# FFN 1's second pair as eight products, setup stores behind the next pair, rescaling on ScalarE, three low parts on Pool

## The reference, cut to what matters

```python
def rmsnorm(x, g):
    return x * lax.rsqrt(jnp.mean(x * x, axis=-1, keepdims=True) + NORM_EPS) * g

def swiglu(x, w_gate, w_up, w_down):
    return (jax.nn.silu(x @ w_gate) * (x @ w_up)) @ w_down

x = x + 0.5 * swiglu(rmsnorm(x, p['g_ffn1']), p['ffn1_gate'], p['ffn1_up'], p['ffn1_down'])
```

## Time and profile before

| | us |
|---|---|
| median of 3 runs | 2503.97 |
| lowest and highest | 2502.36, 2505.84 |
| the profiled execution | 2505.05 |
| its span, first to last instruction | 2503.3 |
| first FFN, pairs 0 to 21 | 8.58 to 551.17 |
| its down side | 552.63 to 808 |

### The profile page before, as it was taken

One profiled execution on the slowest core, in us unless ns is written; L12 is line 12 of the kernel. 1 busy time (PEld: TensorE's weight loads), 2 busy tenths in 40 slices (PEclk: granted clock), 3 DMA queues, 4 the chain that ended last, 5 costly groups with the idle time before them and its releaser, 6 DMA issues. The chain is left out here.

```text
span 2503.3 us, 51841 instructions
## 1 busy us (share of the span) xinstructions
PE 2390.7 (96%) x21940; PEld 2332.1 (93%) x21940; DVE 1441.7 (58%) x1993; ACT 708.5 (28%) x1347; POOL 1193.3 (48%) x761
## 2 busy tenths in 40 slices
PE   7988988899999999999998999999999999999998
PEld 7988988889999999999997888799999999999997
DVE  7787767698226445473357667666754444453225
ACT  6322222230102000011244666522433333341001
POOL 5665666564444334422341000234677778775550
PEclk9999999999999999999999999999999999999998
DMA  5211222243323352543362110054222222153211
GB/s 195 88 68 67 76 76 76 76 185 130 104 78 126 111 119 85 179 89 86 117 202 97 32 33 19 3 211 146 77 85 76 76 76 76 67 186 112 74 51 69
DMA packets 104135, 243.89 MB, mean 97 GB/s; under 512 B 17240, under 2 KB 43480, under 8 KB 103328
## 3 DMA queue, kind: packets, MB, share of 16 engines
q1 hardware_dynamic: 76560, 190.72, 22.8%
q10 hardware_dynamic: 27408, 50.76, 6.4%
HBM read 174.47 MB, written 65.82 MB: 96 GB/s over the span
## 5 line engine op out<-in xcount | busy, mean ns | idle before, releaser
L172 POOL TENSOR_TENSOR whi<-wraw,small 128x1024 fp32r<-128x1024 f32 (+1 forms) x60 | 103.4, 1724 | 418.4 <-PE ps L206 340.1
L921 PE MATMUL ps<-t_hi,whi 128*128 128x258 f32 x688 | 151.5, 304 | 54.5 <-POOL wlo L494 25.7
L206 PE MATMUL ps<-hhi,whi 128*128 128x344 f32 x816 | 177.4, 326 | 0.0
L206 PE MATMUL ps<-hlo,whi 128*128 128x344 f32 x816 | 174.0, 322 | 0.0
L206 PE MATMUL ps<-hhi,wlo 128*128 128x344 f32 x816 | 173.7, 322 | 0.0
L921 PEld LDWEIGHTS ps<-t_hi,whi 128*128 128x128 f32 x688 | 116.2, 207 | 58.9 <-POOL wlo L494 28.7
L494 POOL TENSOR_TENSOR wlo<-weights_sum,whi 128x512 fp32r<-128x512 f32 x63 | 85.8, 1363 | 135.8 <-ACT whi L761 135.1
L921 PE MATMUL ps<-t_lo,whi 128*128 128x258 f32 x688 | 148.1, 299 | 0.0
L175 POOL TENSOR_TENSOR wlo<-wraw,whi 128x1024 fp32r<-128x1024 f32 (+1 forms) x60 | 145.0, 2416 | 4.7
L921 PE MATMUL ps<-t_hi,wlo 128*128 128x258 f32 x688 | 147.2, 297 | 0.0
L3916 PE MATMUL ps<-t_hi,whi 128*128 128x258 f32 x704 | 143.8, 285 | 3.0 <-ACT ffn_gate L3823 1.0
(11 more groups left out here) (587 smaller groups left out, 6890.7 us busy)
## 6 DMA issues: line engine op xcount, KB each, us to landing
weights_raw_b<-ffn_up SPq DMA_DIRECT2D x22, 1024.0 KB, 5.0
wraw<-ffn_up SPq DMA_DIRECT2D x21, 1024.0 KB, 5.0
a_spilled<-ffn_gate SPq DMA_DIRECT2D x40, 516.0 KB, 2.7
a_raw<-a_spilled SPq DMA_DIRECT2D x40, 516.0 KB, 4.1
wraw<-ffn_down SPq DMA_DIRECT2D x48, 384.0 KB, 3.2
wraw<-w_mix SPq DMA_DIRECT2D x18, 512.0 KB, 3.5
gates<-gate_out ACTq DMA_DIRECT2D x16, 516.0 KB, 3.1
wraw<-w_gates SPq DMA_DIRECT2D x16, 512.0 KB, 3.8
```

Of the source, the lines that this page charges most:

```text
L172: pool.tensor_tensor(g.whi[:, s, 0:n], g.wraw[:, s, 0:n], g.zero.to_broadcast([P, n]), ALU.add).then_inc(g.w_hi, 1)
L206: last = pe.matmul(g.ps[:, 3 * bank_set + b, 0:BLK], w[:, s, k * P:(k + 1) * P], x(k, b), start=(k == 0 and first), stop=(k == kt - 1 and ...
L921: last = pe.matmul(g.ps[:, b0 + c, 0:QB], w(k), x[:, k, c * QB:(c + 1) * QB], start=start and k == 0 and fresh, stop=k == DT // 2 - 1 and ...
```

## The change

- Pair 1 is computed as eight plain products too (`FIRST_PROD[1]`), on the inputs that pair 0 used; its weights are four parts (`FIRST_PARTS`, in a new order) without sums, made high by ScalarE and low by Pool as soon as pair 0 is through with the slot. The broadcasts of `rstd` stand ahead of the eighth product, the last of them behind it. VectorE's root is computed in one go after the mixing; of pair 1 VectorE makes two sums instead of four. ScalarE makes all nine row squares before `t2`.
- The four scalings of x's even late tiles go from Pool to ScalarE; Pool's low parts of `t4` come after the parts of pair 1.
- ScalarE stores a finished setup part at the end of the pair (of the unit, behind its `tile_high`) instead of at the start.
- `PAIR_NS` goes from 5000 to 3300, `DOWN_NS` from 4000 to 2600.
- The low parts of tiles 3 to 5 of the down side's first block go from VectorE to Pool, between the splits of units 0 and 1; TensorE waits for them on `t4_lo`.

The core of the diff (left out: semaphore counts, moved waits, and the removed lines that the new blocks replace on TensorE):

```diff
-FIRST_PARTS = ((3, 0, 0), (0, 1, 0), (1, 0, 1), (2, 1, 1))
-FIRST_PROD = ((0, "b11", 2, True, None), (1, "b11", 0, True, None), (2, "b21", 4, True, None), (3, "b21", 6, True, None),
-              (0, "t1", 2, False, "p1"), (1, "t1", 0, False, "q1"), (2, "b22", 2, False, None), (3, "b22", 0, False, None))
+FIRST_PARTS = ((1, 0, 0), (0, 1, 0), (3, 0, 1), (2, 1, 1))
+FIRST_PROD = (((0, "b11", 2, True, None), (1, "b11", 0, True, None), (2, "b21", 4, True, None), (3, "b21", 6, True, None),
+               (0, "t1", 2, False, (0, "p1")), (1, "t1", 0, False, (0, "q1")), (2, "b22", 2, False, None),
+               (3, "b22", 0, False, None)),
+              ((0, "b11", 2, True, (0, "g2")), (1, "b11", 0, True, (0, "u2")), (2, "b21", 4, True, None),
+               (3, "b21", 6, True, None), (1, "t1", 0, False, (1, "q1")), (0, "t1", 2, False, (1, "p1")),
+               (3, "b22", 0, False, None), (2, "b22", 2, False, None)))
...
-        for n, (s, r, c) in enumerate(FIRST_PARTS):
-            pool.wait_ge(g.st_hi, n + 1)
-            pool.tensor_tensor(place(g.wlo, s), part(0, r, c), place(g.whi, s).bitcast(F32), ALU.subtract)\
-                .then_inc(g.st_lo, 1 if n < 3 else 4)
+        for pair in range(2):
+            for n, (s, r, c) in enumerate(FIRST_PARTS):
+                pool.wait_ge(g.st_hi, 7 * pair + n + 1)
+                pool.tensor_tensor(place(g.wlo, s), part(pair, r, c), place(g.whi, s).bitcast(F32), ALU.subtract)\
+                    .then_inc(g.st_lo, 1 if n < 3 else 4)
         for q in range(4):
-            pool.wait_ge(g.b_mixed, q + 1)
-            pool.tensor_scalar(g.x[:, 2 * q, late], g.x[:, 2 * q, late], gain(2 * q), None, ALU.mult).then_inc(g.b_scaled, 1)
-
-        def low_t4():
-            for q in range(4):
-                pool.wait_ge(g.b_hi, FIRST_HI.index(("t4", q)) + 1)
-                hi, low = g.hb["t4"]
-                pool.tensor_tensor(low[:, q, :], g.x[:, 2 * q + 1, early], hi[:, q, :].bitcast(F32), ALU.subtract)\
-                    .then_inc(g.t4_lo, 1)
-
-        one(0, 0, 1, low_t4)
...
+            if u == 0:
+                for t in range(3, 6):
+                    hi, low, full = g.slot[t]
+                    pool.wait_ge(g.d_hi, t + 1)
+                    pool.tensor_tensor(low[:, :], full[:, :], hi[:, :].bitcast(F32), ALU.subtract).then_inc(g.t4_lo, 1)
...
-        G1, U1 = halved(g.gate, 1), halved(g.upv, 1)
-        done(v, 0, 1, 3)
-        g.fst_copy.wait(v, 0, 1, "p1")
-        on(v.tensor_tensor(G1[0], two("y", 1), G1[0], ALU.add))
         first_root()
-        done(v, 0, 1, 4)
-        g.fst_copy.wait(v, 0, 1, "p5")
-        on(v.tensor_tensor(U1[1], two("x", 1), U1[1], ALU.add))
         newton()
         newton()
         v.sem_inc(g.rstd_small, 1)
-        done(v, 0, 1, 5)
-        g.fst_copy.wait(v, 0, 1, "u2")
-        on(v.tensor_tensor(G1[1], two("z", 1), G1[1], ALU.add))
-        for n in range(2):
+        G, U = halved(g.gate, 1), halved(g.upv, 1)
+        done(v, 0, 1, 2)
+        g.fst_copy.wait(v, 0, 1, "p1")
+        on(v.tensor_tensor(G[0], banks(4), G[0], ALU.add))
+        g.fst_copy.wait(v, 0, 1, "q1")
+        on(v.tensor_tensor(U[0], banks(6), U[0], ALU.add))
+        for n, (c0, c1) in enumerate(((0, 512), (512, SEQ), (SEQ, TOK))):
             v.wait_ge(g.rstd_b, n + 1)
-            v.tensor_copy(g.rstd[:, 512 * n:512 * (n + 1)], g.ps[:, 6 + n, :]).then_inc(g.rstd_ready, 1)
-        done(v, 0, 1, 6)
-        on(v.tensor_copy(U1[0], two("x", 1)))
-        v.wait_ge(g.rstd_b, 3)
-        v.tensor_copy(g.rstd[:, SEQ:TOK], g.ps[:, 6, 0:NB]).then_inc(g.rstd_ready, 1)
+            v.tensor_copy(g.rstd[:, c0:c1], g.ps[:, 6 + n % 2, 0:c1 - c0]).then_inc(g.rstd_ready, 1)
...
-            if last:
-                tile_low(3)
...
-                tile_low(4)
-                tile_low(5)
+                v.sem_inc(g.d_lo, 3)
...
-        for n in range(4):
+        for q in range(4):
+            x = g.x[:, 2 * q, late]
+            act.activation(x, x, ACT.Copy, scale=gain(2 * q)).then_inc(g.b_scaled, 1)
+        first_part(1, 0)
+        rows_squares(0)
+        rows_squares(1)
+        first_part(1, 1)
+        rows_squares(2)
+        rows_squares(3)
+        done(act, 0, 0, 5)
+        on(act.activation(G[1], banks(2), ACT.Copy))
...
+        first_part(1, 2)
+        rows_squares(4)
+        done(act, 0, 0, 6)
+        on(act.activation(U[1], banks(0), ACT.Copy))
+        first_part(1, 3)
+        for n in range(5, ROWS):
             rows_squares(n)
-        hi_of(7, 0)
-        act.wait_ge(g.xt_sq, 4)
-
-        def t2(q):
+        G, U = ([halves(t[:, 1, x]) for x in xa] for t in (g.gate, g.upv))
+        act.wait_ge(g.b_lo, FIRST_LO.index(("t1", 3)) + 1)
+        done(act, 0, 1, 0)
+        on(act.activation(G[0], banks(2), ACT.Copy))
+        done(act, 0, 1, 1)
+        on(act.activation(U[0], banks(0), ACT.Copy))
+        act.wait_ge(g.xt_sq, ROWS)
+        for q in range(4):
             act.wait_ge(g.b_mixed, 4 + 2 * q + 2)
             high("t2", q, g.x[:, 2 * q, early])
-
-        t2(0)
-        t2(1)
-        done(act, 0, 0, 5)
-        on(act.activation(G[1], banks(2), ACT.Copy))
-        hi_of(8, 0)
-        t2(2)
-        t2(3)
-        done(act, 0, 0, 6)
-        on(act.activation(U[1], banks(0), ACT.Copy))
-        hi_of(9, 0)
-        rows_squares(4)
-        G, U = ([halves(t[:, 1, x]) for x in xa] for t in (g.gate, g.upv))
-        done(act, 0, 1, 0)
-        act.wait_ge(g.b_lo, FIRST_LO.index(("t1", 3)) + 1)
-        on(act.activation(G[0], two("x", 1), ACT.Copy))
-        hi_of(10, 0)
         for q in range(4):
-            act.wait_ge(g.b_mixed, 4 + 2 * q + 1)
             high("t3", q, g.x[:, 2 * q, late])
-        done(act, 0, 1, 1)
-        on(act.activation(U[1], two("z", 1), ACT.Copy))
-        rows_squares(5)
-        rows_squares(6)
-        done(act, 0, 1, 2)
-        on(act.activation(G[1], two("x", 1), ACT.Copy))
-        rows_squares(7)
-        rows_squares(8)
-        act.wait_ge(g.xt_sq, ROWS)
-        hi_of(11, 0)
         for q in range(4):
             act.wait_ge(g.b_mixed, 12 + q + 1)
             high("t4", q, g.x[:, 2 * q + 1, early])
-        for n in (12, 13, 14, 15):
-            hi_of(n, 0)
-
-        def full_silu(j, n):
+        hi_of(14, 0, 10)
+        hi_of(15, 0, 11)
+        done(act, 0, 1, 5)
+        on(act.activation(U[1], banks(0), ACT.Copy))
+        done(act, 0, 1, 6)
+        on(act.activation(G[1], banks(2), ACT.Copy))
+
+        def full_silu(j):
             g.fst_up.wait(act, 0, j, "gm")
-            on(act.activation(g.gate[:, j, :], g.gate[:, j, :], ACT.Silu), n)
+            on(act.activation(g.gate[:, j, :], g.gate[:, j, :], ACT.Silu))
...
-            setup["scalar"](act, pair)
...
+            setup["scalar"](act, pair)
         for u in range(LAST):
             b, k = divmod(u, DT)
-            setup["scalar"](act, NP + u)
             if k < down_size(b + 1):
                 tile_high(FIRST_BLOCKS[b + 1][0] + k)
+            setup["scalar"](act, NP + u)
...
+        for pair in range(2):
+            for n, (p, name, b0, start, copied) in enumerate(FIRST_PROD[pair]):
+                s = FIRST_PARTS[p][0]
+                pe.wait_ge(g.st_lo, 7 * pair + (p + 1 if p < 3 else 7))
+                if copied:
+                    g.fst_copy.wait(pe, 0, *copied)
+                if pair and n in (2, 3):
+                    g.fst_up.wait(pe, 0, 0, ("g1a", "u1a")[n - 2])
+                last = multiply(lambda k: place(g.whi, s, k), lambda k: place(g.wlo, s, k), name, b0, start, pair == 0)
+                if n != 2:
+                    last.then_inc(g.st_done, 1)
+                if pair and n == 6:
+                    pe.wait_ge(g.rstd_small, 1)
+                    g.fst_up.wait(pe, 0, 1, "u1a")
+                    pe.wait_ge(g.c_in, 16 * 3)
+                    rate(range(8))
+        pe.wait_ge(g.rstd_ready, 1)
+        rate((8,))
...
+                if u == 0 and n > 2:
+                    pe.wait_ge(g.t4_lo, 4 + n - 2)
+                else:
+                    pe.wait_ge(g.d_lo, f + n + 1)
...
-PAIR_NS, DOWN_NS = 5000, 4000
+PAIR_NS, DOWN_NS = 3300, 2600
```

More of the change, by code:

```diff
@@ L497, in total, with one @@
             pool.tensor_tensor(out, x, y, op).then_inc(g.fst_sum.sem, 1)
-        def one(i, b, j, between=None):
+        def one(i, b, j):
             pair, n = 2 * b + j, 7 * j
@@ L646, in _ @@
             gate, up = g.gate[:, j, :], g.upv[:, j, :]
-            if j == 0:
-                g.fst_copy.wait(v, 0, 0, "u2")
-                g.fst_up.wait(v, 0, 0, "u1a")
-            else:
-                g.fst_up.wait(v, 0, 1, "u1")
+            g.fst_copy.wait(v, 0, j, ("u2", "g2")[j])
+            g.fst_up.wait(v, 0, j, "u1a")
             on(v.tensor_tensor(gate, gate, g.rstd[:, :], ALU.mult))
@@ L731, in _, with on, first_part @@
     def _(act):
-        def on(ins, n=1):
-            ins.then_inc(g.fst_copy.sem, n)
+        def on(ins):
```

(46 more changed lines are left out.)

29 lines of the change are left out of this document (15 added, 14 removed).

## The result

| us | before | after |
|---|---|---|
| median of 4 runs | 2504.90 | 2464.59 |
| lowest and highest | 2502.36, 2507.73 | 2461.24, 2466.70 |
| the profiled execution | 2505.05 | 2466.70 |
| its span | 2503.3 | 2464.9 |
| pair 1 | 34.26 to 72.20 | 34.28 to 69.95 |

The ratio of the medians is 0.984, 95% interval 0.982 to 0.986: 40 us faster, where 51 were forecast. The time of 2464.6 lies inside the range of 2428 to 2467, near its upper end.

What follows compares the result with a forecast made beforehand. TensorE, busy 96% of the span, bounds the kernel, so only idles and low clock can be won. Terms -49.0 (pairs 2 to 21), -2.1, +3.5, -3.5 sum to -51.1 us: median 2452.9, range 2428 to 2467.

Steps and rivals of the forecast that it cites:

- pair 1: First FFN's pair 1 as eight products: broadcasts wait 7.8 us for VectorE's late root; gain 2.1 us, bounds 0 and 12.6.
- start of the down side: Three low parts moved to Pool delay unit 1's split: loss 3.5 us, bounds 1 and 6.
- down units: Down projection's setup budget of 2600 ends the overrun in units 4 to 7: gain 3.5 us.
- Rival B: Pair 1: the root isn't late, VectorE gets its steps in between; pair costs 25.3 us, total 2442; 8%.
- case B: Pairs 9, 12, 14, 15, 17, 18, 20: ScalarE waits at a setup store, delaying Pool's low part and product 2; 25.7 us.
- case A: Pairs 4, 6, 8, 10, 16, briefly 20: VectorE's setup slot delays the sum before product 6; 4.22 us idle in pair 4.
- rival D: Pool's instructions, not VectorE's count, set the slot: even pairs 4 to 20 each lose 7.2 us; total 2513; 3%.
- Budget, pairs 4 to 10: Even pairs: slot of 19 instructions lasts 13.2 us, idle falls from 4.22 to 2.33 us, 4.3 us lost each, 17.2 in all.
- rival A: Even pairs' slots end in time, 19 instructions costing 10.2 us; remaining 23 us go too, total 2430; 15%.
- Budget, pairs 12 to 20: Even pairs: 12 and 14 lose 0.5 us each; 16, 18 and 20 idle 1.3 to 2.0 us, losing 2.2 each.
- The clock behind the idles: Pairs with a TensorE idle: an idle of 2.35 us costs 4.0 us in all, as read from pair 15.
- Rival C: Down projection's setup overruns in all its 21 units: 9.37 us instead of 8.49 in 19 of them; total 2473; 8%.

Runs made afterwards that it cites:

- the early root: Kernel after, with VectorE's root in pair 1 moved ahead of the low parts of t2: 2456.45 us, ratio 0.981.
- the uneven budgets: Kernel after, with the setup budget of 3300 behind each pair made 4600 behind even and 1900 behind odd pairs: 2432.32 us, ratio 0.971.
- the kernel with all that helped: Kernel after plus root ahead of t2's low parts, budgets 4600/1900, and low parts of tiles 3 to 5 back on VectorE: 2425.27 us, repeated 2421.50.

## Why the prediction was right, and where it was off

By its own steps, in us against the kernel before, from the two profiled executions:

| step | predicted | measured |
|---|---|---|
| pairs 2 to 21 | -49.0 | -37.4 |
| pair 1 | -2.1 | -2.3 |
| start of the down side | +3.5 | +2.7 |
| down units | -3.5 | -3.6 |
| rest of the kernel | 0 | +2.2 |
| span | -51.1 | -38.4 |

**Pair 1.** Right in its mechanism and its numbers: the broadcasts began at 62.26 (62.2 predicted) after 7.63 us of waiting (7.8), and pair 2 at 69.95 (70.1). Rival B's 25.3 us for pair 1 are the true length without the wait, as the early root shows; only the order of VectorE's instructions stood in the way. The root's steps were taken to come one per Pool instruction, and eight of the twelve took over 1.1 us.

**Stores.** Right: case B's idles of 25.7 us for Pool's low part are gone, and with the stores moved alone its even pairs turn into case A, as rival D said of them.

**Budget, pairs 4 to 10.** Right. VectorE's timeline of pair 4 in the kernel after, and of pair 12 with the last instruction of Pool's run:

```profile
119.10 1.27 DVE L1042 TENSOR_SCALAR s_par<-s_par 128x16 f32<-128x16 f32 x1
...
132.17 0.17 DVE L1042 TENSOR_SCALAR s_par<-s_par 128x16 f32<-128x16 f32 x1
132.38 0.69 DVE L662 TENSOR_TENSOR ffn_gate<-ps,ffn_gate 128x516 f32<-128x516 f32 x1
...
298.52 1.39 DVE L1101 TENSOR_TENSOR s_tmp<-s_par,s_in_part 128x128 f32<-128x128 f32 x1
...
306.03 1.41 DVE L1101 TENSOR_TENSOR s_tmp<-s_par,s_in_part 128x256 f32<-128x256 f32 x1
...
310.09 1.29 POOL L501 TENSOR_TENSOR weights_sum<-weights_sum,weights_raw_b 128x512 f32<-128x512 f32 x1
310.13 1.33 DVE L1095 TENSOR_TENSOR s_tmp<-s_par,c_raw 128x64 f32<-128x64 f32 x1
```

The slot of nineteen took 13.2 us, as taken from the earlier trace rows, and the idle is 2.35 us against 2.33. The four pairs lost 17.8 us against 17.2. That their sum fits so well is in part luck: with the same idle, pair 4 took 23.12 us under the early root, at a clock of 1.00, and 24.35 in the kernel after. Reading the slot's end from the row of its 19th instruction was right, where the proportion (10.2 us, rival A) would have promised 23 us more.

**Budget, pairs 12 to 20.** Here the sum failed, in size and not in kind. The step reads: "Those in pairs 12 and 14 hold 10 wide ones; the tenth of that width ended 9.9 us into its slot". That row was of pair 10, where the first five of the ten were half as wide (128x64) and three took 0.23 to 0.29 us. In pair 12 nine of the ten took 1.08 to 1.42 us each and the slot 12.9 us, where 10.9 was taken as harmless: idles of 2.04 and 1.05 us, 4.3 us lost in the two pairs and not 1.0. In pairs 16, 18 and 20 the idles came out at 2.41, 2.16 and 2.13 us, above the 1.3 to 2.0 predicted, and in 16 and 20 the clock fell as well: 11.5 us lost, not 6.6. What the step missed is that a slot's length follows the Pool instructions that it meets more than its own number. In pairs 12 to 20 Pool runs nine instructions beside each slot, and eight or nine of VectorE's take over 1 us, whether the slot holds 10, 14 or 15, as in the slot of nineteen; the slots of 14 and 15 last 13.0 to 13.3 us. What falls away with a smaller number are cheap ones, in Pool's short break and behind its run. So rival D's mechanism held in part, from nineteen instructions down to ten. It did not hold from 28 to nineteen, where nine cheap ones went, nor for the slots of 5 to 12 under the uneven budgets, which met six to eight Pool instructions and lasted 7.3 to 10.8 us.

**Pair 2.** "Pair 2's 2.0 us hang on a spill and stay": the idle grew from 1.64 to 2.45 us, because pair 2 now begins 2.25 us sooner and the spill only some 1.4 sooner; ScalarE's copy starts at 77.78 where it started at 79.23. With that the clock fell (0.93) and the pair lost 4.1 us, not 2.0.

```profile
77.78 0.60 ACT L851 ACTIVATE ffn_gate<-ps 128x516 f32<-128x516 f32 x1 [4.53 <-DMA a_spilled<-ffn_gate]
```

The terms add up: 0.6 in pairs 4 to 10, 3.3 in 12 and 14, 4.9 in 16 to 20, 2.1 in pair 2 and 0.6 of low clock in pairs 5, 7 and 21 make 11.5 of the 11.6 us missing.

**The clock behind the idles.** The cost was taken as 4.0 us for an idle of 2.35, from pair 15. In the kernel after the pairs with an idle fall into two sorts. Those at a clock of 0.93 or 0.94 (2, 4, 6, 8, 10, 16, 20) lost 4.1 to 4.6 us with idles of 2.1 to 2.5; those at 1.00 (12, 14, 18) lost their idle and 0.6 more. Pairs 12 and 16 changed sorts between two kernels with the same idles. Even one kernel does not settle it. The two traces of the kernel with all that helped have an idle of 3.47 and 3.44 us in pair 2, and this pair took 26.77 us in one and 25.39 in the other:

```profile
59.46:86.23 26.77, 23.30 (x170) 23.09 (x169) 15.00 (x13) 11.03 (x17) 18.70 (x13) 0.87 0.26 98
59.63:85.02 25.39, 21.95 (x170) 21.75 (x169) 14.00 (x13) 10.93 (x17) 19.79 (x13) 0.93 0.30 108
```

Which sort a pair falls into was not found out; what was wrong in the prediction is that it took the size of the idle for the thing that decides.

**Down side.** Right. Unit 1 waits for Pool's split (1.63 us), units 4 to 20 take 8.5 us, and the start lost 2.7 us, within its bounds of 1 and 6. The two waits for the low parts came to 1.06 and 1.11 us. Rival C, an overrun in every unit, did not occur: VectorE is busy for 26.8 of 34 us in units 4 to 7.

**Rest of the kernel.** The 2.2 us are within the spread of this part over the traces, 1691.7 to 1699.7. One place that differs is the stretch from 842.5 to 856.2, where the clock was 0.50 for 13.7 us; before, the like stretch from 883 to 899 had a mean of 0.79, some 6.7 us at the lower level. By an estimate from these two the stretch alone is worth 3.5 us. What sets it was not looked into.

## What to carry to other kernels

Price filler work on VectorE by the Pool instructions that it meets and not by its own duration, and give the filler to the stretches where Pool has gaps: here the same list of instructions in uneven portions gained another 32 us, where the whole change of five edits had gained 40. When a dependent chain of tiny instructions can stand in an idle time ahead of Pool's work, put it there first (2.4 us against 10.7). And after removing a wait, look one step further along for the transfer or the eviction that was hidden behind it, as pair 2's spill was.
